# Attention of the second block by features: values stationary on column halves, normalised probabilities, another order of steps

## The reference

```python
def second_block(x, ...):
    for i in range(DEPTH):                                  # DEPTH = 2
        h = rms_norm_2(x, attn_norm_g[i])
        q, k, v, u, vv = jnp.split(h @ w_in[i], split_at, axis=-1)   # 512, 128, 128, 512, 512
        q = axial_rope(rms_norm_2(q.reshape(b, s, 8, 64), q_norm_g[i]), tables)
        k = axial_rope(rms_norm_2(k.reshape(b, s, 2, 64), k_norm_g[i]), tables)
        attn_o = gqa_attention(q, k, v)                     # softmax(q k^T / 8) v, 8 heads on 2 k/v heads
        sg_o = spatial_gating(jax.nn.gelu(u), jax.nn.gelu(vv), ...)
        merged = jnp.concatenate([rms_norm_2(attn_o, attn_out_g[i]),
                                  rms_norm_2(sg_o, sg_out_g[i])], axis=-1)
        x = x + merged @ w_o[i]
        ...                                                 # FFN with a convolution over tokens
```

## Time and profile before

| | us |
|---|---|
| median of 3 runs (1457.5 to 1457.8) | 1457.58 |
| the profiled execution | 1457.24 |
| its span | 1455.9 |
| TensorE busy | 1437.5 (99%) |
| VectorE busy | 1038.3 (71%) |
| ScalarE busy | 809.2 (56%) |
| GpSimd busy | 64.7 (4%) |
| chain that ended last | 92% TensorE, 4% VectorE |

### The profile page before, as it was taken

The page is one execution under the profiler, slowest core; times in us unless marked ns, Lnnn a source line. Parts: engine busy times, 40 slices in busy tenths (PEclk is TensorE's granted clock), DMA queues, the critical chain, the costliest instruction groups (busy, mean ns, idle before and its releaser), DMA issues.

```text
span 1455.9 us, 19709 instructions
## 1 busy us (share of the span) xinstructions
PE 1437.5 (99%) x7731; PEld 1209.7 (83%) x7731; DVE 1038.3 (71%) x1417; ACT 809.2 (56%) x1159; POOL 64.7 (4%) x100
## 2 busy tenths in 40 slices
PE   6999999999999999999999999999999999999999
PEld 5888887888888788887888888788888888888888
DVE  5656885855557656885866556877988868788886
ACT  3556644445543555755354444676665567765563
POOL 2000000000001000000010000210000012000000
PEclk9999999999999999999999999999999999999999
DMA  8654644575565654552756655436566644456651
GB/s 297 213 182 149 216 145 134 167 234 189 179 208 192 203 165 151 190 172 87 235 181 222 199 192 184 132 109 220 167 188 200 224 125 168 131 179 201 200 186 58
DMA packets 172477, 261.08 MB, mean 179 GB/s; under 512 B 9313, under 2 KB 111361, under 8 KB 172129
## 3 DMA queue, kind: packets, MB, share of 16 engines
q1 hardware_dynamic: 170944, 254.13, 53.8%
q0 software_dynamic: 1152, 4.65, 1.0%
q10 hardware_dynamic: 288, 1.05, 0.2%
HBM read 256.65 MB, written 1.05 MB: 177 GB/s over the span
## 4 chain that ended last, share of the span: by engine, by line
PE 92%; DVE 4%; ACT 1%; POOL 1%; DMA 1%; issue 0%; SPq 0%; DVEq 0%; ACTq 0%
PE ps L441 16%; PE ps L512 12%; PE ps L514 11%; PE ps L513 11%; PE ps L442 9%; PE ps L411 6%; PE ps L415 6%; PE ps L413 6%; PE ps L444 2%; DVE wlo L1664 1%; PE ps L811 1%; PE ps L469 1%; DVE x L1683 1%; DVE x L1681 1%; PE ps L616 1%; DMA raw<-in_w_in 1%
## 5 line engine op out<-in xcount | busy, mean ns | idle before, releaser
L1664 DVE TENSOR_TENSOR wlo<-raw,whi 128x2048 fp32r<-128x2048 f32 (+1 forms) x238 | 528.5, 2229 | 223.9 <-ACT whi L1168 223.9
L1168 ACT ACTIVATE whi<-raw 128x2048 fp32r<-128x2048 f32 (+1 forms) x238 | 442.2, 1866 | 150.7 <-PE ps L514 52.7
L441 PE MATMUL ps<-xT,whi 128*128 128x512 f32 x1008 | 356.4, 395 | 0.0
L442 PE MATMUL ps<-xT,wlo 128*128 128x256 f32 x1152 | 311.2, 280 | 0.0
L512 PE MATMUL ps<-whi,xT 128*128 128x512 f32 (+3 forms) x640 | 250.5, 391 | 3.8 <-DVE xT L1690 1.3
L514 PE MATMUL ps<-whi,xT 128*128 128x512 f32 (+3 forms) x640 | 242.0, 378 | 0.0
L513 PE MATMUL ps<-wlo,xT 128*128 128x512 f32 (+3 forms) x640 | 241.3, 377 | 0.0
L441 PEld LDWEIGHTS ps<-xT,whi 128*128 128x128 f32 x1008 | 189.0, 188 | 42.2
L442 PEld LDWEIGHTS ps<-xT,wlo 128*128 128x128 f32 x1152 | 217.4, 189 | 6.1
L512 PEld LDWEIGHTS ps<-whi,xT 128*128 128x128 f32 x640 | 120.3, 188 | 27.4 <-issue 4.4
L514 PEld LDWEIGHTS ps<-whi,xT 128*128 128x128 f32 x640 | 120.2, 188 | 22.5
(11 more groups left out here) (236 smaller groups left out, 1943.2 us busy)
## 6 DMA issues: line engine op xcount, KB each, us to landing
raw<-in_w_in SPq DMA_DIRECT2D x124, 512.0 KB, 4.7
raw<-in_w_ffn_in SPq DMA_DIRECT2D x88, 512.0 KB, 4.9
raw<-in_w_up SPq DMA_DIRECT2D x88, 512.0 KB, 4.8
raw<-in_w_ffn_out SPq DMA_DIRECT2D x44, 512.0 KB, 4.5
raw<-in_w_down SPq DMA_DIRECT2D x44, 512.0 KB, 4.4
raw<-in_w_branch SPq DMA_DIRECT2D x24, 512.0 KB, 4.7
raw<-in_w_out SPq DMA_DIRECT2D x16, 512.0 KB, 4.2
raw<-in_w_o SPq DMA_DIRECT2D x16, 512.0 KB, 4.6
```

The source lines that it names most:

```text
L441: PE.matmul(ps[:, b, :], hi, m.xT[:, kt], start=kt == 0, stop=False)
L442: mm = PE.matmul(ps[:, b, 0:S], lo, m.xTh[:, kt], start=False, stop=False)
L1168: AC.activation(m.whi[:, i % SPLIT, 0:w], m.raw[:, slot, 0:w], ACT.Copy).then_inc(s.w_hi, 1)
L1664: DV.tensor_tensor(m.wlo[:, i % SPLIT, 0:w], m.raw[:, slot, 0:w], m.whi[:, i % SPLIT, 0:w].bitcast(F32), ALU.subtract).then_inc(s.w_lo, 1)
```

## The change

All of it is in the second block's layers.

- TensorE's mix (`mix_weights`) keeps a 128 x 64 block of values stationary, one head on each half of the columns, and moves 256 tokens of transposed probabilities: 4 matmuls a pair for 8. The outputs come features first, so `turn_outputs` goes. Its steps are in the order scores, queries, fill, transposes, fill, transposes, fill, mix.
- VectorE normalises the past pair's probabilities at the start of a step (`normalise_pair`), and `turn_weights` waits for that (`probs_in`). `heads_out` goes.
- ScalarE copies the first transposed head between a step's two exponentials, and the second after them, with the split behind it.
- `weighted_hi` squares the mix into `gate` and makes the high half with the gain, `weighted_lo` the low half. The sum of squares over features: GpSimd adds the four pairs' squares, TensorE multiplies the sum with a column of ones, once for each half of the tokens, in front of the fourth k-tile of the first output half, VectorE copies the two columns.
- Features are now ordered by pairs, so the gain's columns (`pairs`) and the rows of `w_o` (`load_pairs`, two DMAs, each to 64 partitions) follow.

```diff
+        for g in range(1, 4):
+            PO.wait_ge(s.o_squared, 4 * L + g + 1)
+            if g > 1:
+                PO.wait_ge(s.o_summed, n["summed"])
+            PO.tensor_tensor(o_squares(0), o_squares(0), o_squares(g), ALU.add).then_inc(s.o_summed, 1)
+            n.up("summed")
         rsqrt(s.out_sq, *rows(24, 2), 1.0 / 512, RMS_EPS, out=s.out_root)
...
         def turn_weights(i):
 
-            PE.wait_ge(s.exped, h0 + i + 1)
+            PE.wait_ge(s.probs_in, p0 + i + 1)
...
+        def mix_weights(g):
+
+            PE.wait_ge(s.probs_out, p0 + 2 * g + 2)
+            if m0 + g:
+                PE.wait_ge(s.pair_out, m0 + g)
+            for kt in range(2):
+                for j in range(2):
+                    mm = PE.matmul(ps[64 * j:64 * j + 64, 7, (g % 2) * S:(g % 2 + 1) * S],
+                                   m.proj[:, kt, 640 + 64 * j:704 + 64 * j], m.probT[:, j, kt * S:(kt + 1) * S],
+                                   start=kt == 0, stop=kt == 1)
+            mm.then_inc(s.pairs_mixed, 1)
...
             if g < 3:
                 turn_queries(g + 1).then_inc(s.qk_turned, 1)
-            if g == 3:
-                PE.wait_ge(s.pair_out, m0 + 2)
-                PE.wait_ge(s.qk_out, g0 + 4)
-                turn_outputs((0, 2), 6)
+            fill(g, 1)
+            if g:
+                turn_weights(2 * g - 2)
             fill(g, 2)
             if g:
...
+                turn_weights(2 * g - 1)
             fill(g, 3)
+            if g:
+                mix_weights(g - 1)
...
+            if (th, kt) == (0, 3):
+                PE.wait_ge(s.o_summed, 3 * L + 3)
+                for h in range(2):
+                    mm = PE.matmul(ps[:, 6, h:h + 1], m.gate[:, 0, 1152 + h * P:1152 + (h + 1) * P], m.ones[:, 0:1], start=True,
+                                   stop=True)
+                mm.then_inc(s.o_sum, 1)
...
+    def weighted_hi(m0, g):
+        AC.wait_ge(s.pairs_mixed, m0 + g + 1)
+        o = ps[:, 7, (g % 2) * S:(g % 2 + 1) * S]
+        AC.activation(m.gate[:, g // 2, 1152 + g % 2 * S:1152 + g % 2 * S + S], o, ACT.Square).then_inc(s.o_squared, 1)
+        AC.activation(m.aTh[:, g, :], o, ACT.Copy, scale=m.pcol[:, g:g + 1]).then_inc(s.pair_hi, 1)
...
+                if g and not j:
+                    probs_out(p0, 2 * g - 2, m0 + g - 1)
+            catch(2, L, "at", g, 2, ahead=0)
+            if g:
+                probs_out(p0, 2 * g - 1, m0 + g - 1)
+            split_to(rounded[g])
             catch(2, L, "at", g, 3, ahead=0)
+            if g:
+                weighted_hi(m0, g - 1)
...
         for g in range(5):
+            if g:
+                normalise_pair(h0, g - 1)
...
             split_to(rounded[g])
             catch(2, L, "at", g, 3, ahead=0)
+            if g:
+                weighted_lo(g - 1)
         catch(2, L, "at", 5, 0, ahead=0)
         split_to(s0 + 4)
         catch(2, L, "at", 5, 1)
+        DV.wait_ge(s.o_sum, L + 1)
+        DV.tensor_copy(m.small[:, 24:26], ps[:, 6, 0:2]).then_inc(s.out_sq, 1)
```

More of the change, by code:

```diff
@@ L44 @@
     ("probT", [P, 2, 2 * S], F32), ("ident", [P, P], F32),
-    ("rope", [P, 2, 112], F32), ("half", [P, 16], F32), ("small", [P, 64], F32),
+    ("rope", [P, 2, 112], F32), ("half", [P, 16], F32), ("ones", [P, 2], F32), ("small", [P, 64], F32),
     ("bn", [P, 2, 2, 6], F32), ("mv", [P, 2, 2], F32), ("rs", [P, 8, 2], F32), ("ri", [P, 8, 2], F32),
@@ L287, in sync_program @@
                     load_piece(w2[:, kt:kt + 4, c0:c0 + 512], 4, 512)
-        for kts in ((4, 8), (0, 4)):
-            for j in range(2):
-                load_block(t["w_o_2"][L], kts, j * 512, 512)
+        for j in range(2):
+            load_block(t["w_o_2"][L], (4, 8), j * 512, 512)
+        for j in range(2):
+            load_pairs(t["w_o_2"][L], j * 512, 512)
         load_ffn(2, t["w_up_2"], t["w_down_2"], L)
@@ L321, in rows, with o_squares @@
         return m.small[:, o:o + w], m.half[:, 0:w]
+    def o_squares(g):
+        return m.gate[:, g // 2, 1152 + g % 2 * S:1152 + g % 2 * S + S]
     PO.wait_ge(s.init, 1)
@@ L1018, in turn_weights @@
             mm.then_inc(s.probs_turned, 1)
+        def mix_weights(g):
[3 more added lines that the diff above has]
+            for kt in range(2):
+                for j in range(2):
+                    mm = PE.matmul(ps[64 * j:64 * j + 64, 7, (g % 2) * S:(g % 2 + 1) * S],
+                                   m.proj[:, kt, 640 + 64 * j:704 + 64 * j], m.probT[:, j, kt * S:(kt + 1) * S],
+                                   start=kt == 0, stop=kt == 1)
+            mm.then_inc(s.pairs_mixed, 1)
         fill(0, 0)
         for g in range(5):
-            if g:
-                turn_weights(2 * g - 2)
-            fill(g, 1)
-            if g:
-                turn_weights(2 * g - 1)
             if g < 4:
@@ L1906, in rotate, with weighted_lo @@
         return DV.tensor_tensor(x2, x2, tmp1, ALU.add)
[L1908 to L1913 removed]
+    def weighted_lo(g):
+        DV.wait_ge(s.pair_hi, n.up("pair_hi"))
+        DV.scalar_tensor_tensor(out=m.aTl[:, g, :], in0=ps[:, 7, (g % 2) * S:(g % 2 + 1) * S], scalar=m.pcol[:, g:g + 1],
+                                in1=m.aTh[:, g, :].bitcast(F32), op0=ALU.mult, op1=ALU.subtract).then_inc(s.pair_out, 1)
+    DV.memset(m.ones[:], 1.0)
     DV.memset(m.half[:], -0.5).then_inc(s.init, 1)
@@ L2190, in queries_out @@
             DV.tensor_copy(m.qk[:, g % 2, 0:w], ps[:, 6, 0:w]).then_inc(s.qk_out, 1)
-        def heads_out(g):
-            DV.wait_ge(s.pairs_mixed, m0 + g + 1)
-            then(DV.reciprocal(m.ri[:, 2 * g:2 * g + 2, :], m.rs[:, 2 * g:2 * g + 2, :]))
-            for th in range(2):
-                a = DV.tensor_tensor(m.proj[:, th, O2:O2 + 512].rearrange("p (j g d) -> p j g d", j=2, g=4)[:, :, g, :],
-                                     ps[:, 7, th * P:(th + 1) * P].rearrange("p (j d) -> p j d", j=2),
-                                     m.ri[:, 2 * g:2 * g + 2, th].unsqueeze(2).broadcast_to([P, 2, 64]), ALU.mult)
-            a.then_inc(s.pair_out, 1)
         queries_out(0)
```

75 lines of the change are left out of this document (18 added, 57 removed).

## The result

The changed kernel takes 1483.7 us (median of 5 runs, 1479.7 to 1484.9) against 1457.54 (5 runs), a ratio of 1.0174, interval 1.0162 to 1.0186: slower by 26.2 us. The forecast was 1478.8, 21.3 slower, its range 1469 to 1489.

A forecast was written before the change was run, and what follows sets the result against it. TensorE was taken as the bound, busy 1437.5 of 1455.9 us. Per layer, 14.2 us of waits less 0.3 already there and 3.25 less work gives 10.65, +21.3 for two: 1478.8 us, range 1469 to 1489.

The forecast's parts named there:

- What leaves TensorE: Second block's attention: mix 2.8 us less, output transposes 1.0 less, sum of squares 0.55 more; net 3.25 less a layer.
- What waits: TensorE's waits in a second-block attention stage, from laying four engine queues side by side: 14.2 us a layer, 0.3 there before.
- step 1 first: Step 1's first transposes of probabilities wait 3.2 us for VectorE's vv products, split and normalising of one head.
- step 2 first: Step 2's first transposes wait 1.4 us for VectorE's split, low half and normalising.
- step 3 first: Step 3's first transposes wait 0.9 us for square and copy on ScalarE, then low half and normalising.
- step 4 first: Step 4's first transposes wait 1.05 us for the chain of square, copy, low half and normalising.
- tail: Stage end, transposes of x: TensorE waits 1.3 us, as VectorE's sum copy and the root delay the residual add.
- Step 1 second: Step 1's second transposes wait 1.3 us for the rest of the normalising, maximum, exponentials and ScalarE's copy.
- The granted clock falls in the gaps: Rival: TensorE at half rate after a stage's longest gap, up to 6 us a layer more, 1491 us; chance 0.06.
- The cover: Rival: new waits stay at 0.3 us a layer, so the kernel gains 6.5 us, 1451; chance 0.03.
- Half the waits: Rival: queues close up and waits are half the forecast's, +7 us, 1465; chance 0.07, and 0.02 for ending within 0.2%.
- Columns that don't share: Rival: column halves don't share the array, so the new mix costs what the old did, 1484 us; chance 0.02.

The follow-up runs named there:

- no_norm: Changed kernel without the second block's division of probabilities by their sums; transposes wait for the exponentials alone. 1473.24 us, ratio 1.0115.
- busy: Changed kernel with throwaway transposes of the identity on TensorE in its waits at the transposes of probabilities. 1476.88 us, ratio 1.0135.
- gap: Kernel before, with one added TensorE wait for VectorE's vv products in each second-block layer, ahead of step 1's first transposes. 1466.76 us, ratio 1.0059.
- order_only: Changed kernel in the old order of steps, without the division; VectorE copies the mix, sum copied between the last two splits. 1458.41 us, ratio 1.0006.
- no_norm_first: Changed kernel without the division, first probability copy ahead of both exponentials, sum copied between VectorE's last two splits. 1472.18 us, ratio 1.0103.
- split_behind: Changed kernel with VectorE normalising a pair in the step of its exponentials, ahead of that step's split of weights. 1479.93 us, ratio 1.0148.
- rows_early: Changed kernel in the old order; early reciprocal sums over 256 columns, spread by two transposes, multiply the mix; sum copied between last splits. 1463.35 us, ratio 1.0040.

## Why the prediction was right, and where it was off

**What leaves TensorE: right, as work.** The mix takes 1.02 us, forecast 1.01. The sum's four records hold TensorE 0.36 us from start to start (997.67 to 998.03), forecast 0.55. In no_norm, with the clock full, TensorE is busy 4.4 us less than before, against 6.5.

**What waits: right in place, too long in size.** The forecast's list against the first layer of the changed kernel: step 1 first 2.77 for 3.2, step 2 first 0.72 for 1.4, second 1.60 for 1.75, step 3 first 0.46 for 0.9, second 2.04 for 2.2, step 4 first 0.52 for 1.05, tail 0.75 and another 0.64 at the first output matmul of the next bank for 1.3, start 0.39 for 0.4. Step 1 second has no wait of its own here, since TensorE was slow behind the first; in busy there are 1.09 us, forecast 1.3. Of the waits at the mix (0.2 and 0.5) only one shows, 0.20 in busy. By group, a layer: 4.1 us for VectorE's normalising where the forecast had 6.5, 4.0 for ScalarE's copies where it had 6, and 1.4 at the transposes of x for 1.3. The slow clock shortens them, since TensorE comes later; the next paragraph takes them without it.

**The sum: a little too long.** At full clock (busy) a stage takes 64.2 where the layout had 65.15, and the kernel 19.5 us more than before where it had 21.3. It lies inside the bounds given, 18.7 to 23.8 (the upper one is 24.3 by its own terms, 2 x (15.7 - 0.3 - 3.25)). But this is two errors that offset each other. With their filling counted in, the waits of busy's first layer add up to 12.2 us for 14.2, 11.9 of them new, and the stage is 9.7 longer than before (64.2 for 54.5). That leaves 2.2 us a layer for the shorter work, where the forecast had 3.25; no_norm's 4.4 for both layers says the same. What took the other 1.0 was not found: the mix and the sum of squares are as forecast or better. The waits that were too long are the first transposes of all steps, by some 0.3 each (2.93, 1.06, 0.61 and 0.68 for 3.2, 1.4, 0.9 and 1.05), the second of step 1 by 0.2, and those at the mix by 0.5. For steps 3 and 4 the chain of square, copy and low half was laid too long: in busy the low half is done at 973.4, forecast 973.95.

**The clock: the step that failed.** "The granted clock falls in the gaps" had a chance of 0.06, since the gaps "are 3 us at most, with work between". They were 2.8, and it fell: in the first layer in two stretches (behind waits of 2.77 and 2.04 us), in the second in three (behind waits of 2.76, 2.05 and 2.00 us). It adds 6.7 us. The size given, "up to 6 us a layer", was nearly reached in the second layer (5.5 above busy's stage) and missed in the first, which with two falls is only 1.4 above: in gap a fall costs 1.6 us, and it costs less where TensorE would have waited next anyway. So the nearness of the forecast, within 5 us, is in part luck: waits too long by 3.9 us, a gain in work too large by 2.1, and the clock's 6.7 left out. The run of 1479.67, closest to the forecast, is no better proof of it: it has some of the clock's part in it.

The Trainium skill, "TensorE: Matmul & The Clock Gate", section "HAM oscillation", which has gaps of TensorE throttle its clock again, was the better guide here than the absence of long gaps in the trace of before; busy and gap bear it out. The gaps that this section warns of are longer than any here; in these runs some of 2.0 to 3.3 us were enough, and others as long were not.

**The rivals.** The cover did not hold: the waits at the transposes of probabilities alone are 16.3 us, 8 a layer, where the change would have needed less than 3.5. Half the waits: no. Columns that don't share: no, 1.02.

**What the single causes are worth.** Against busy's 64.2 a stage at full clock: the normalising in front of the transposes 2.3 to 2.8 (no_norm; its layout had 4.0); the order of steps, by order_only against no_norm_first, about 6.9 with the clock in it, some 5 to 6 without (an estimate: 6.9 less up to 1.64); what TensorE has less in the mix comes back as waits, even in the old order. These don't add up cleanly, since each wait removed lengthens the one behind it; split_behind showed that best (7.1 us off VectorE's waits, 7.0 onto ScalarE's). Which part of the order matters most, the scores ahead of the transposes or the exponentials ahead of the copies, was not separated.

No version beats the kernel before. The nearest that computes the same is rows_early, 5.9 us behind it.

## What to carry to other kernels

Before making the busiest engine's work shorter, ask which chains of the other engines its present work just covers: here TensorE got some 2 us a layer less to do (4.0 in all, by its busy time), and none of it shortened the kernel, even in the old order (there 0.7 us a layer of new waits came from my placing of the squares). An operation put in front of a consumer (a division ahead of transposes) costs the whole queue that stands ahead of it on its engine, a 2.2 us split here, not its own 0.7 us; moving it only shifts the wait to the next chain, so edits must be laid out together. And a kernel whose TensorE never rests can pay for a new gap of 2 to 3 us twice, once for the wait and once for the clock behind it: give it throwaway work there as a test, and the difference is the clock's share.

## What the runs showed of the hardware

- A gap of 3.09 us in an otherwise full TensorE was followed by the clock at half in one layer and not in the other of the same execution; gaps of 2.77, 2.05 and 2.00 were followed by it too (changed kernel), while one of 3.29 (split_behind, first layer; in its second the same wait was), two of 2.81 (no_norm) and one of 2.36 (changed kernel, second layer) were not. When it fell, it was at 0.50 for 3 to 4 us, once for nearly 7 (1236.8 to 1243.6 in the changed kernel), rows of 512 columns 0.43 us apart for 0.23, and one fall cost 1.64 us unhidden (gap). This is what made executions of one kernel differ by 5 us (1479.7 to 1484.9) where the kernel before differs by 0.5.
- Transposes of the identity in the gaps (128 columns, 0.12 us each) kept the granted clock at 1.000 in every execution of two kernels.
- VectorE's reciprocal takes 0.17 us on 4 columns and 1.75 on 256, where a copy of 256 from PSUM takes 0.42.
- GpSimd's add of 128x256 took 0.8 us (two in 1.61), but the last of the three in each layer of the changed kernel 2.44, and the second in order_only and rows_early 2.54. A split of VectorE, with two inputs from SBUF, ran beside each of the long ones (989.23 to 991.52 beside 989.68 to 992.12); whether it is the cause was not tested.
